# A fused decoder layer: the second tile's output projection and the query weights moved around the expert gathers, with a gather ring of four, then six buffers

## What is computed

```python
x += hybrid_mixer(rmsnorm(x))              # 8 MoBA heads and 8 FoX heads of 64, then w_out
x += memory_cross_attention(rmsnorm(x))    # 4 heads of 256: w_xq, softmax, w_xo
h  = rmsnorm(x)                            # peer_ffn, per token, for each of 8 routing heads:
qr = (h @ w_query).reshape(C, 8, 2, 64)
s1, s2 = qr[:, :, 0] . sub_keys_1, qr[:, :, 1] . sub_keys_2       # 128 scores each
v1, i1 = top_k(s1, 16); v2, i2 = top_k(s2, 16)
cand   = v1[:, None] + v2[None, :]                                # 256 candidate sums
top_s, pos = top_k(cand, 16)
eidx   = i1[pos // 16] * 128 + i2[pos % 16]                       # 16 of 16384 experts
y += sum_e softmax(top_s)_e * gelu(h . expert_down[eidx_e]) * expert_up[eidx_e]
out = rmsnorm(x + y)
```

## Time and profile before

| | |
|---|---|
| runs | 929.0, 930.4, 935.2 us; median 930.4 |
| profiled execution | 936.0 us, span 934.2 us |
| busy, share of the span | PE 88%, PEld 50%, DVE 60%, ACT 48%, POOL 26% |
| gathers | 256, 268.45 MB, 69.9% of the 16 DMA engines' span |
| other loads and stores (SP and ACT) | 47.3 MB |
| granted TensorE clock | 0.975 on average |

### The profile page before, as it was taken

One profiled execution on the slowest core, in us unless ns is written; L12 is line 12 of the kernel. 1 busy time (PEld: TensorE's weight loads), 2 busy tenths in 40 slices (PEclk: granted clock), 3 DMA queues, 4 the chain that ended last, 5 costly groups with the idle time before them and its releaser, 6 DMA issues.

```text
span 934.2 us, 9666 instructions
## 1 busy us (share of the span) xinstructions
PE 822.9 (88%) x3215; PEld 463.4 (50%) x3215; DVE 557.5 (60%) x1348; ACT 443.8 (48%) x1088; POOL 242.4 (26%) x267
## 2 busy tenths in 40 slices
PE   8999999999999899888899899977778787877885
PEld 7999996787565365344343455432223222222222
DVE  5545342213457766776757657776767666676543
ACT  5435554334134645665536645463553535445343
POOL 0000000000023333334333333433334343333430
PEclk9999999997999899999999999989999999999999
DMA  9897532070099999999999999999999999999994
GB/s 335 221 313 251 193 113 91 1 269 2 1 371 414 392 418 416 402 413 413 408 390 423 421 422 408 405 403 410 422 422 419 423 420 423 421 414 422 417 422 202
DMA packets 64337, 316.28 MB, mean 339 GB/s; under 512 B 7908, under 2 KB 12069, under 8 KB 31525
## 3 DMA queue, kind: packets, MB, share of 16 engines
q0 software_dynamic: 36864, 268.45, 69.9%
q1 hardware_dynamic: 26348, 45.70, 13.8%
q10 hardware_dynamic: 1080, 1.59, 1.1%
HBM read 313.10 MB, written 2.62 MB: 338 GB/s over the span
## 4 chain that ended last, share of the span: by engine, by line
PE 51%; DMA 31%; ACT 10%; DVE 6%; issue 2%; POOL 0%; POOLq 0%; ACTq 0%
DMA qkvb<-in_expert_rows,expert_idx 19%; PE y L1319 14%; DMA spare<-in_expert_rows,expert_idx 12%; PE v_bank L1319 6%; PE h_psum L1095 5%; PE v_bank L1085 5%; PE a_bank L1085 4%; PE a_bank L1095 4%; PE v_bank L1095 3%; PE h_psum L1085 3%; DVE qkvb L1023 3%; PE v_bank L1184 2%; ACT diag L730 2%; ACT L723 2%; DVE spare L1023 1%
## 5 line engine op out<-in xcount | busy, mean ns | idle before, releaser
L555 POOL DMA_INDIRECT qkvb<-in_expert_rows,expert_idx x172 | 161.9, 941 | 539.3 <-DVE expert_idx L1006 259.0
L723 ACT ACTIVATE gelu<-dots,stat 128x1 f32<-128x1 f32 x256 | 75.2, 294 | 315.1 <-DVE dots L1023 314.4
L1319 PE MATMUL v_bank<-qkvb,diag 128*128 128x512 f32 x344 | 173.1, 632 | 48.9 <-ACT diag L730 48.9
L1319 PE MATMUL y<-qkvb,diag 128*128 128x512 f32 x344 | 165.6, 620 | 18.1 <-ACT diag L730 18.1
L1023 DVE CUSTOM_DVE_ANT_0 qkvb<-a_bank,qkvb 128x1024 f32<-128x1024 f32 x86 | 105.2, 1224 | 74.6 <-DMA qkvb<-in_expert_rows,expert_idx 74.6
L1023 DVE CUSTOM_DVE_ANT_0 qkvb<-h_psum,qkvb 128x1024 f32<-128x1024 f32 x86 | 105.0, 1223 | 61.1 <-DMA qkvb<-in_expert_rows,expert_idx 61.1
L1319 PEld LDWEIGHTS v_bank<-qkvb,diag 128*128 128x128 f32 x344 | 61.1, 194 | 160.4 <-ACT diag L730 111.4
L555 POOL DMA_INDIRECT spare<-in_expert_rows,expert_idx x84 | 78.9, 939 | 131.9 <-PE y L1319 69.3
L1319 PEld LDWEIGHTS y<-qkvb,diag 128*128 128x128 f32 x344 | 63.9, 196 | 99.0 <-issue 58.3
L730 ACT ACTIVATE diag<-ident,wgt 128x128 f32<-128x128 f32 x256 | 102.7, 401 | 8.3
L1319 PE MATMUL v_bank<-spare,diag 128*128 128x512 f32 x168 | 81.8, 613 | 19.5 <-ACT diag L730 19.5
(11 more groups left out here) (209 smaller groups left out, 1154.9 us busy)
## 6 DMA issues: line engine op xcount, KB each, us to landing
weights<-in_w_in SPq DMA_DIRECT2D x5, 2048.0 KB, 33.1
weights<-in_w_xk SPq DMA_DIRECT2D x2, 2048.0 KB, 17.0
weights<-in_w_xv SPq DMA_DIRECT2D x2, 2048.0 KB, 10.7
weights<-in_w_out SPq DMA_DIRECT2D x2, 2048.0 KB, 8.7
weights<-in_w_xq SPq DMA_DIRECT2D x2, 2048.0 KB, 7.9
weights<-in_w_xo SPq DMA_DIRECT2D x2, 2048.0 KB, 11.4
weights<-in_w_peer_query SPq DMA_DIRECT2D x2, 2048.0 KB, 17.7
qkvb<-in_expert_rows,expert_idx POOLq DMA_INDIRECT x172, 10.1
```

What stands on the lines that cost most here:

```text
L555: pool.indirect_dma_start(ROWS[n % NS], None, expert_rows, bass.IndirectOffsetOnAxis(ap=IDX[:, H % 3, k:k + 1], axis=0))\
L723: nc.scalar.activation(gel[:, i:i + 1], dots[:, i:i + 1], ACT.Gelu, scale=rms("root_p", n // SPT)).then_inc(gelu_done, 1)
L1319: ins = nc.tensor.matmul(YP[t][:, b * BLK:(b + 1) * BLK], diag[:, i, :], ROWS[i][:, D + b * BLK:D + (b + 1) * BLK], start=False, stop=last)
```

## The change

- **Loads.** Query block 0 goes to `spare` as before and stays there for both tiles; block 1 goes to the second half of `qkvb` (v and bias), as soon as the last attention head is done. The two loads into `weights` are gone.
- **Ring.** Buffers 0 and 1 are the first half of `qkvb`, 2 and 3 lie in `weights` 1, which holds w_out's half 1, 4 and 5 in `weights` 0 with half 0. Up to slot 11 gathers go round four buffers, from slot 12 (`GROWN`) round six. Gather 2 waits for `wout` (1,1), gather 16 for `wout` (1,0).
- **Tile 1's projection.** `wout` (1,1) stands whole behind the first routing scores; `wout` (1,0) is cut into quarters behind slots 1, 3, 6 and 8.
- **First routing.** `("top", 0, 0)` chooses ranks 0 to 7 first and lets gathers 0 to 7 go, then ranks 8 to 15. In every head the copy of the scores ahead of the search is gone.
- **FFN gain.** `xg` is gone; x is transposed as it is and DVE multiplies by the gain as it copies out (`gained`).
- **Table of slots.** Quarters of `wq` (0,1), `xq` and `xo` stand two per five slots instead of one per two, `wq` (1,i) stay; cross-attention's heads stand four slots apart instead of five.
- The ten products on the identity ahead of slot 0 are gone.

```diff
-    main += [("xo", 0, 0), ("oT", 1, 0), ("xg", 0, 0), ("oT", 1, 1), ("xo", 0, 1), ("xg", 0, 1), ("pT", 0, 0)]
-    main += rest[1][:1] + [("square_p", 0, 0), ("pT", 0, 1), ("start", 0, 0), ("wq_first", 0, 0), ("y_start", 0, 0),
-                           ("sc_first", 0, 0), ("sc_first", 0, 1), ("root_p", 0, 0), ("top", 0, 0), ("y_start", 0, 1)]
-    main += rest[1][1:] + [("wq", 0, 0), ("sc", 0, 0), ("sc", 0, 1)] + rest[0]
+    main += [("xo", 0, 0), ("oT", 1, 0), ("oT", 1, 1), ("xo", 0, 1), ("pT", 0, 0), ("y_start", 0, 0), ("square_p", 0, 0),
+             ("pT", 0, 1), ("start", 0, 0), ("wq_first", 0, 0), ("sc_first", 0, 0), ("sc_first", 0, 1),
+             ("y_start", 0, 1), ("root_p", 0, 0), ("top", 0, 0)]
+    main += rest[1] + [("wq", 0, 0), ("sc", 0, 0), ("sc", 0, 1)]
...
-             ((19, 21, 23, 25), ("xq", 1, 0)), ((27, 29, 31, 33), ("xq", 1, 1))]
+             ((25, 27, 30, 32), ("xq", 1, 0)), ((35, 37, 40, 42), ("xq", 1, 1))]
...
+    def buffer(n):
+        return n % NB if n < GROWN else n % NS
+    def users(n):
+        return [m for m in range(n) if buffer(m) == buffer(n)]
...
+    CHOICE = ("pairs", "ones", "picks", "experts")
+    FIRST_TOP = TOP[:8] + tuple("first " + part for part in CHOICE) + TOP[8:11] + tuple(
+        "last " + part for part in CHOICE) + TOP[15:]
...
-        ROWS = [QKVB[:, 2 * i:2 * i + 2, :].rearrange("p a x -> p (a x)") for i in range(NB)]
-        ROWS += [SPARE[:, 2 * i:2 * i + 2, :].rearrange("p a x -> p (a x)") for i in range(NS - NB)]
+        ROWS = [QKVB[:, 2 * i:2 * i + 2, :].rearrange("p a x -> p (a x)") for i in range(2)]
+        for b in (1, 0):
+            ROWS += [W[:, SLOT[("w_out", b)], 2 * D * i:2 * D * (i + 1)] for i in range(2)]
...
-            for b in (1, 0):
-                load_block("w_peer_query", b)
+            for b in range(2):
+                if b == 1:
+                    sp.wait_ge(o_full, 2 * T)
+                sp.dma_start(w_query[b], A["w_peer_query"][0].rearrange("(k p) c -> p k c", p=P)
+                             [:, :, b * BLK:(b + 1) * BLK]).then_inc(ld_query[b], 16)
...
-                if n == NB:
-                    pool.wait_ge(a_full, AN[("wq", 0, 0)] + 1)
-                if n >= NS:
-                    pool.wait_ge(up_used, n - NS + 1)
+                if n == 2:
+                    pool.wait_ge(*full(("wout", 1, 1)))
+                if users(n):
+                    pool.wait_ge(up_used, users(n)[-1] + 1)
+                elif n >= GROWN:
+                    pool.wait_ge(*full(("wout", 1, 0)))
...
-                        after(t_mark(nc.vector.tensor_copy(sc[:, :, :].rearrange("p a x -> p (a x)"), scores)))
...
-            hold = bank_for(slots[0][1])
-            for _ in range(10):
-                nc.tensor.matmul(hold[:, 0:P], ident[:, :], ident[:, :], start=True, stop=True)
```

144 lines of the change are left out of this document (71 added, 73 removed).

## The result

The kernel before took 929.3 us in the median of 20 runs, the changed one 936.1 (20 runs): a ratio of 1.0064, 95% interval 1.0045 to 1.0083. The ratio leaves out one run of 949.4 us, at a lower clock. The changed kernel is 0.6% slower, some 6 us, where 6.4 us of gain were forecast. The profiled execution took 941.2 us (span 939.3).

A forecast was written before the change was run, and what follows sets the result against it. From the first expert gather on, the DMA byte stream at 420 GB/s was taken as the bound. 3.4 by row 17, 0.2 after it and 2.9 from pacing made 6.5, taken as 6.4: 930.4 to 924.0 us, range 916 to 930.

The forecast's parts named there:

- The start: Before the gather stream: search at 250.2, first gather near 256.7, first `up` near 267.4, 7.5 us earlier, two slow `up`s.
- row 17: Yardstick row, counted from 0, after which both kernels run six buffers: forecast to land at 313.5, 3.4 us ahead of 316.9.
- a sign against it: At the first `up`s: the forecast is wrong if the low clock lasts beyond two `up`s.
- The ring of four: Slots up to row 17: landing 5.4 plus 4.6 makes 10.0 us a round, 2.50 a slot, no slack; eats 9.1 us.
- the walk: Slots 0 to 17 stepped through with forecast durations: row 4 at 276.8, row 5 at 279.8, row 17 at 313.5.
- a full stream's lead: Up to row 17: with no holes it would land at 304.4, 12.5 us ahead, 10.0 of that from bytes.
- the hole ahead of the first release: Between rows 3 and 4: `up` 0 ends at 271.2, so row 4 lands only at 276.8, a hole of 4.7 us.
- rival 3: TensorE stays at the low clock through the ring of four, 1.7 us a slot; fifteen slots give 949; chance 0.06.
- Bytes: Head of the stream: two 2 MB query loads leave it, 4.19 MB, 10.0 us, the largest thing the change can give.
- After row 17: Stall from 310 to 325 goes from 1.6 to 1.4 us; 560 to 600 keeps 1.6; six buffers hide added table loads.
- The pacing: Two quarters per five slots, 2.41 us a slot instead of 2.58: closes holes at 460 to 500 and 360 to 380, 2.9 us.
- The sum: Whole kernel: 3.4 + 0.2 + 2.9 = 6.5 us gained, taken as 6.4; forecast chance 0.53 for a gain of 4 to 9.

The follow-up runs named there:

- wq_later: Changed kernel with tile 1's last query product quarters moved to slots 114, 115, 117, 118, its scores behind slot 123; ratio to before 1.0047.
- quiet gauge: `ring_gauge`: kernel before with POOL held to four gathers ahead for gathers 140 to 179, five for 180 to 219; 949.8 us, run once.
- ring_six: Changed kernel with six buffers from gather 4 on, half of tile 1's output projection multiplying a `w_xq` block; 927.5 us, 0.9992 of before.
- xq_later: Changed kernel with the cross-attention query quarters moved from slots 25 to 42 to slots 29 to 44; ratio to before 1.0083, 6 runs.
- pacing_alone: Kernel before with only tile 1's cross-attention quarters two per five slots instead of one per two; 0.9991 of before.

## Why the prediction was wrong, point by point

**The start: right.** The key search began at 250.3 (250.2 forecast), the first gather went at 257.05 (256.7), the first `up` at 267.9 (267.4), and two `up`s were slow. The two slow `up`s cost 1.8 us here (2.9 in `wq_later`) and not the 3.3 of the earlier trace rows, and at row 17 nothing that can be seen. The low clock did come back beyond them, which the forecast had named as a sign against it (below).

**The ring of four: the first step that failed.** The prediction took 5.4 us for every landing, called it that of a lone gather, and so got a round of 10.0 us and 2.50 us a slot, "just the pace of the bytes". The reading of the earlier trace rows was wrong in a small way: its two gathers were issued at 318.9 and 321.8, 2.9 us apart, so they were not alone. The step was wrong in a larger one: in the ring of four the landing takes longer. The views by line give, for the gather issued at 271.87 with nothing else under way, for the next one at 273.59, and for all issued from 271 to 305:

```profile
DMA to landing us min/median/max: 5.6/5.6/5.6
...
DMA to landing us min/median/max: 7.8/7.8/7.8
...
DMA to landing us min/median/max: 5.4/7.5/8.4
```

The quiet gauge gives a median of 6.7 and 2.86 us a slot. By the estimate of the Trainium skill's page that the prediction weighed (DMA: Bandwidth & Descriptors, Anatomy of one DMA) it would have been 4.4; the trace contradicts this already for the gather with nothing else under way (5.6), and more in the ring. In the walk the error shows from slot 5 on: row 4 was forecast at 276.8 and its dot ran at 277.5, row 5 at 279.8 and 281.4. `up` 11 was to end at 301.2 and ended at 304.9, and row 17 at 313.5 came at 317.8. From row 4 to row 17 that is 40.2 us where 36.7 were forecast; 11 gathers at 0.36 us over the forecast pace make 4.0 by the gauge, so this term alone is of the size of the miss.

Of a full stream's lead the ring was to eat 9.1 us. After the mark, a full stream would bring row 17 at 11.8 + 5.4 + 17 x 2.49 = 59.5; it came at 72.5, so 13 us were eaten. `ring_six` gives 10.2 of these back: 3.8 by row 4, the hole ahead of the first release, which the forecast had (4.7), and 6.4 from there on, of which the gauge's pace explains about 4. The other 2 or so are open. `up`s 5 and 6 and a quarter at 283.8 to 293.1 are at the low clock (0.66 there, some 3 us over their usual length together), and the table loads of a softmax lie in the same slots; `ring_six` has neither a wait nor a slow product in these slots. But `xq_later` and `wq_later`, the same program up to there, have only one slow `up`, 1.7 us over, and row 17 comes at 71.7 and 72.9 in them. So a part of the prediction's rival 3 was there, and its share isn't shown.

**Bytes: right as an account, wrong as a ranking.** "The largest thing the change can give", 10.0 us, gave 2.1 by itself. The forecast put fewer bytes and earlier gathers together as 12.5 us for a full stream; with six buffers 8.9 us of it are real at row 17 (71.2 less 62.3). That the first `up`s and quarters of TensorE are a second bound of nearly the same length as the bytes was not seen, though the trace of before had it. In its table by stretches both are full at once:

```profile
285.00:290.00 5.00, 5.00 (x32) 3.81 (x31) 2.64 (x8) 1.65 (x5) 1.65 (x3) 1.00 1.02 412
```

**After row 17: the second step that failed, two waits put at nothing.** The prediction named the slot table's effect on gates, softmaxes and table loads but not on the banks of `a_bank`. It kept the hole of 560 to 600 at its old 1.6 us. Slots 112 to 124 take 4.3 more, of which `wq_later` gives 3.3 back; slots 17 to 36 take 3.7 more, and moving the quarters takes 2 to 5 away. By the stretches of the two profiles these two, 8.0 us, are more of the miss than the ring's 4.7.

**The pacing: right and larger in its stretch, not shown in the whole.** 2.9 us were forecast; 36 to 84 takes 119.7 to 122.3 us in all seven executions that have it, and 124.7 to 126.8 in the five that have not, some 4 to 5 us. By itself, though, it gave the whole 0.9991 (0.9968 to 1.0014). The exponentials four slots apart cost nothing that can be seen: 120.7 us with them, 121.5 with five slots in `pacing_alone`.

**The sum.** Forecast: 3.4 + 0.2 + 2.9 = 6.5 won. Measured by the stretches: 1.3 lost up to row 17 (instead of 3.4 won, 4.7 off), 3.7 and 4.3 lost at the bank waits, 5.1 won by the pacing, 1.3 lost elsewhere. The middle of 6.4 missed by 12 us. In the prediction's terms: the ring took 4.7 us more than forecast and the two waits 8.0 that it had at nothing, and the pacing gave 2.2 more. The class, within 1% of before, was the likeliest one given, but the range ended at 930: rival 3 was the only way to a loss, and it was priced at 949 for another mechanism. A small loss by plain waits was not among the rivals. One sum inside that rival is slightly off as well: nine slow slots of 1.7 us less the gain of 6.4 are 8.9 us, which is still within 1%; it takes ten. And the walk lets `up` 0 end at 271.2, where 267.4 and half of the 6.70 of the earlier trace rows make 270.8.
